# SSM input projections of a decoder step as three products of rounded parts

## The reference

```
cq, ckv, kr, z, xbc, dt, mq, g = split(x @ w_in)      # one input projection
o_mla = latent attention (8 heads) on cq, ckv, kr     # branch A
xbc   = silu(causal_conv(xbc)); y = ssd(xbc, dt) * silu(z); o_ssm = rms(y) # branch B, 4 groups of 8 heads
o_mem = attention of mq into 256 memory tokens        # branch M
m  = sig(gA)*(o_mla@WoA) + sig(gB)*(o_ssm@WoB) + sig(gM)*(o_mem@WoM)
x1 = LN(alpha*x + m@w_out);  y = LN(alpha*x1 + relu(x1@w_up+b)^2 @ w_down + b)
```

## Time and profile before

| | us |
|---|---|
| Median of 3 runs | 1787.76 (1786.57 to 1789.56) |
| The profiled execution's own time | 1788.35 |
| Its span in the trace | 1786.7 |
| PE busy in the span | 1712.9 (96%) |
| DVE / ACT / POOL busy | 734.7 / 379.3 / 370.1 |
| SSM stage, from the first matmul to the end of block 46 | 5.6 to about 495.5 |

### The profile page before, as it was taken

One profiled execution on the slowest core, in us unless ns is written; L12 is line 12 of the kernel. 1 busy time (PEld: TensorE's weight loads), 2 busy tenths in 40 slices (PEclk: granted clock), 3 DMA queues, 4 the chain that ended last, 5 costly groups with the idle time before them and its releaser, 6 DMA issues.

```text
span 1786.7 us, 25145 instructions
## 1 busy us (share of the span) xinstructions
PE 1712.9 (96%) x10132; PEld 1416.8 (79%) x10132; DVE 734.7 (41%) x1284; ACT 379.3 (21%) x758; POOL 370.1 (21%) x330
## 2 busy tenths in 40 slices
PE   8999999999999999999899999999996999999995
PEld 6767667677777877787677777778895999999995
DVE  5565667665341121111222212311157871157345
ACT  2151332514312121111011111100124111111122
POOL 0040221402210000000233210000034433434332
PEclk9999999999999999999999999999999999999998
DMA  5324224252253222221777775432221222222221
GB/s 211 116 77 142 89 78 148 77 174 66 85 192 110 65 61 70 71 71 42 236 232 247 239 256 186 156 106 71 72 95 36 83 89 89 84 94 83 89 78 50
DMA packets 70405, 206.18 MB, mean 115 GB/s; under 512 B 10161, under 2 KB 26802, under 8 KB 65682
## 3 DMA queue, kind: packets, MB, share of 16 engines
q1 hardware_dynamic: 50384, 151.67, 26.3%
q10 hardware_dynamic: 13762, 31.93, 5.2%
q0 software_dynamic: 6144, 20.98, 4.0%
HBM read 189.68 MB, written 14.86 MB: 114 GB/s over the span
## 4 chain that ended last, share of the span: by engine, by line
PE 90%; DVE 5%; DMA 2%; ACT 1%; issue 1%; SPq 1%; POOL 0%; POOLq 0%; ACTq 0%; DVEq 0%
PE acc L1638 37%; PE acc L1678 23%; PE acc L1939 6%; PE acc L1905 3%; PE bank L1849 2%; PE acc L1887 2%; PE acc L2042 1%; PE bank L1954 1%; PE bank L1973 1%; PE bank L1955 1%; PE bank L1809 1%; PE bank L2056 1%; PE bank L1924 1%; PE bank L1930 1%; PE bank L2127 1%
## 5 line engine op out<-in xcount | busy, mean ns | idle before, releaser
L1638 PE MATMUL acc<-xt,ring 128*128 128x272 f32 x2496 | 602.4, 399 | 3.2 <-DMA ring<-in_stream 3.2
L1638 PEld LDWEIGHTS acc<-xt,ring 128*128 128x128 f32 x2496 | 472.9, 192 | 124.6 <-issue 30.0
L485 POOL TENSOR_TENSOR f_parts<-ring,f_parts 128x1024 fp32r<-128x1024 f32 x72 | 173.4, 2409 | 392.7 <-ACT f_parts L662 392.7
L1678 PE MATMUL acc<-x_parts,f_parts 128*128 128x272 f32 x1664 | 236.7, 292 | 16.8 <-DVE x_parts L1085 11.2
L1678 PEld LDWEIGHTS acc<-x_parts,f_parts 128*128 128x128 f32 x1664 | 221.2, 191 | 19.9 <-issue 13.3
L1678 PE MATMUL acc<-f_parts 128*128 128x272 f32 x1536 | 194.3, 289 | 0.0
L1678 PEld LDWEIGHTS acc<-f_parts 128*128 128x128 f32 x1536 | 193.6, 188 | 0.2
L463 POOL DMA_DIRECT2D work<-in_page_cols x128 | 68.8, 538 | 475.1 <-PE bank L1994 365.5
L662 ACT ACTIVATE f_parts<-ring 128x1024 fp32r<-128x1024 f32 x72 | 76.5, 1062 | 336.2 <-PE acc L1678 331.9
L1939 PE MATMUL acc<-branch,ring 128*128 128x272 f32 x512 | 120.0, 392 | 0.0
L1939 PEld LDWEIGHTS acc<-branch,ring 128*128 128x128 f32 x512 | 96.0, 190 | 18.8
(11 more groups left out here) (329 smaller groups left out, 1822.1 us busy)
## 6 DMA issues: line engine op xcount, KB each, us to landing
ring<-in_stream SPq DMA_DIRECT2D x216, 512.0 KB, 3.6
work<-in_page_cols POOLq DMA_DIRECT2D x128, 160.0 KB, 3.4
attended<-in_ssm_state ACTq DMA_DIRECT2D x8, 1024.0 KB, 6.2
work<-cum_rows SPq DMA_DIRECT2D x32, 256.0 KB, 4.5
out_ssm_s<-attended ACTq DMA_DIRECT2D x8, 1024.0 KB, 5.6
work<-in_ckv_rows ACTq DMA_DIRECT2D x64, 128.0 KB, 3.6
work<-in_ckv_rows SPq DMA_DIRECT2D x64, 128.0 KB, 3.0
work<-in_memk_cols SPq DMA_DIRECT2D x8, 1024.0 KB, 6.5
```

What stands on the lines that cost most here:

```text
L485: pool.tensor_tensor(split[j][1], ring[:, s * BLOCK:(s + 1) * BLOCK], split[j][0].bitcast(F), SUB).then_inc(sem["split_ready"], 1)
L1638: m = pe.matmul(acc[p][:, half, 0:width], w[:, k * P:(k + 1) * P], x(kk)[:, half * width:(half + 1) * width], start=kk == 0, stop=kk == n_ ...
L1678: m = pe.matmul(acc_half, w[:, k * P:(k + 1) * P], x[:, kk, of], start=kk == 0 and n == 0, stop=kk == last and n == 2)
```

## The change

The 46 projections of the SSM stage (`project_x` in place of `project`) become three fp32r products as well, 48 matmuls a block in place of 16. Four things come with it.

1. Weights. After each evacuation of an accumulator ACT rounds a block into one of two buffers (`high_part`), and POOL subtracts it from the ring's slot in place (`low_part`). `high_part(n)` stands behind the evacuation of block n-2 and waits until PE has begun block n-1; PE begins block n when `low_part(n)` is done. POOL does 46 such subtractions between its other work.
2. x. Before block 1, ACT rounds the 8 chunks of x (128x544), DVE subtracts (8 operations, ahead of the dt work), and ACT rounds x once more over x itself, chunk by chunk, as PE's dt matmuls have taken each chunk. x is loaded again (2.2 MB, one DMA of SP) after the stage, as is the memory (1 MB, before at 38 us from ACT's queue, now from SP's when the last group's outputs are read out).
3. Buffers. `th` lies on `ext`, `rstd` on `sq_sum`, `b_mask` on `b_tm`. So `evac` of the third conv slice and on waits for the `finish` of the slice two before (`conv_ready`), and POOL's `b_mask` waits for the four state sums.
4. Waits that are merged or renamed (`vec_loaded` into `const_loaded`, `gate_a_ready` into `act_over`); DVE's first operation needs the constants in both kernels.

```
+            def high_part():
+                at = hi_at.next()
...
+                act.wait_ge(sem["blocks_begun"], CREDIT["blocks_begun"] + at)
+                act.wait_ge(sem[f"weights_in_slot{s}"], 16 * (loaded_before(at, s) + 1))
+                act.activation(w_hi[at % 2], ring[:, s * BLOCK:(s + 1) * BLOCK], ACT.Copy).then_inc(sem["hi_ready"], 1)
...
+            def low_part(n=1):
+                for _ in range(n):
...
+                    pool.wait_ge(sem["hi_ready"], t.next("hi_ready"))
+                    pool.tensor_tensor(ring_lo[:, slot], ring[:, slot], w_hi[at % 2].bitcast(F),
+                            SUB).then_inc(sem["split_ready"], 1)
...
             def evac(j):
+                n = evacuated.next()
+                if n > 2:
+                    act.wait_ge(sem["conv_ready"], n - 2)
                 act.wait_ge(sem[f"acc{j}_ready"], t.next(f"acc{j}_ready"))
...
+            for c in range(KC):
+                dve.wait_ge(sem["rounded"], t.next("rounded"))
+                dve.tensor_tensor(XL[:, c, :], X[:, c, :], XL[:, c, :].bitcast(F), SUB).then_inc(sem["normed_even"], 1)
...
+            def project_x(p, between=None):
...
+                pe.wait_ge(sem[f"acc{p}_free"], t.next(f"acc{p}_free"))
+                pe.wait_ge(sem["split_ready"], t.next("split_ready"))
+                for half, of in enumerate(halves):
...
+                    for k in range(KC):
+                        if at == 1 and half == 0:
+                            pe.wait_ge(sem["x_split"], t.next("x_split"))
+                        first, m = products(acc[p][:, half, 0:HT], wh, wl, XH, XL, k, k, KC - 1, of)
...
+            sp.wait_ge(sem["y_ready"], GC * GROUPS)
+            sp.dma_start(mem, mem_t).then_inc(sem["mem_loaded"], 16)
+            load(3)
+            sp.wait_ge(sem["blocks_begun"], CREDIT["blocks_begun"] + SSM_SPLIT + 2)
+            sp.dma_start(X, x_t).then_inc(sem["x0_loaded"], 16)
```

More of the change, by code:

```diff
@@ L136 @@
 SPLIT_FROM = blocks_before("out")
+SSM_SPLIT = blocks_before("mem_k") - 1
 def loaded_before(block, slot):
@@ L180, in sb, with raw @@
             return ctx.enter_context(nc.sbuf_tensor(name, [rows, cols], dt))
-        ring = sb("ring", RING * BLOCK)
+        with ExitStack() as as_loaded:
+            def raw(name, cols):
+                return as_loaded.enter_context(nc.sbuf_tensor(name, [P, cols], F))
+            ring, _, _, xt = raw("ring", RING * BLOCK), raw("at_cst", CW), raw("at_vecs", VW), raw("xt", KC * T)
+        ring_lo = sb("ring_lo", RING * BLOCK, R)
         cst = sb("cst", CW)
         vecs = sb("vecs", VW)
-        xt = sb("xt", KC * T)
+        xt_hi = sb("xt_hi", KC * T, R)
         mark = sb("mark", 2, F, 1)
@@ L248, in accv @@
             return acc[p][0:rows, :, 0:HT]
+        XH, XL = chunks(xt_hi, KC), chunks(ssm_parts, KC)
+        w_hi = [ssm_parts[:, KC * T + j * BLOCK:KC * T + (j + 1) * BLOCK] for j in range(2)]
         k = Carver()
-        ext, cacc, th = ([k(EXT) for _ in range(2)] for _ in range(3))
-        krope, a_rstd = k(T), k(T)
+        ext, cacc = ([k(EXT) for _ in range(2)] for _ in range(2))
+        th = [work[:, j * EXT + 3:(j + 1) * EXT + 3] for j in range(2)]
+        st_conv = k(NC * DEC_BATCH * 3).rearrange("p (c b t) -> p c b t", b=DEC_BATCH, t=3)
+        b_s = k(P, NS)
+        dec_p = k(NB * SSM_HEADS).rearrange("p (c h) -> p c h", h=SSM_HEADS)
+        k.at = 6 * T
+        off_s = k(GW)
+        c_mask = k(DEC_BATCH * NS).rearrange("p (b t) -> p b t", t=NS)
+        ecum_s = k(SSM_HEADS)
+        k.at = 6 * EXT
+        krope = k(T)
+        a_rstd = k(T)
         late_sq = [k(T) for _ in range(2)]
@@ L422, in _ @@
                         NS]), C("bmask").rearrange("p (b t) -> p b t", t=NS), MUL).then_inc(sem["c_masked"], 1)
+                low_part(2)
                 pool.wait_ge(sem["b_tm_read"], t.next("b_tm_read"))
+                pool.wait_ge(sem["add_ready"], t.next("add_ready", NB))
                 if g:
@@ L562, in _ @@
                 load()
-            load(blocks_before("sample") - blocks_before("mem_k"))
+            sp.wait_ge(sem["y_ready"], GC * GROUPS)
[3 more added lines that the diff above has]
+            sp.dma_start(X, x_t).then_inc(sem["x0_loaded"], 16)
+            load(blocks_before("sample") - blocks_before("mem_k") - 3)
             def cached_rows(b):
```

155 lines of the change are left out of this document (104 added, 51 removed).

## The result

| | before | changed |
|---|---|---|
| median of the runs | 1787.28 us (1786.57 to 1789.56, 4 runs) | 1810.48 us (1802.14 to 1812.08, 4 runs; a fifth, not in the median, took 1815.89) |
| ratio | | 1.0126, interval 1.0092 to 1.0161 |
| span of the profiled execution | 1786.7 us | 1800.5 us |

The forecast was 1780 us with a range of 1755 to 1798. The median lies 12 us above the range, and on the other side of no change. Both are used.

The account below looks back on a forecast made before the run. The prediction took PE to bound the kernel. Its terms, +9.3 -4.6 -5.8 -10.5 +2.5 +1.0 = -8.1 us against the profiled 1788.35, gave 1780 us with the median's 0.6 lower; range 1755 to 1798.

Parts of the forecast that it names:

- A group: Walk through one group of the SSM stage: second and third -2.9 us each, first -4.6, last -10.5.
- Clock and the end: PE's clock lowered by waits at group starts, +2.5 us; x's reload after the stage, +1.0; `b_mask`'s wait, nothing.
- the conv before the state additions: DVE's conv between block 12's evacuation and PE's first `state_adds`: longer beside POOL's operations and a subtraction, +1.0 us.
- the term put at nothing: POOL's `b_mask` waiting for the state sums, 25 us before `state_adds` wants it: no cost.
- What the products save: Each of 46 projection blocks takes 6.07 us instead of 7.41, saving 1.35 each, at most 62 us.
- DVE is not stopped: Rival for the SSM stage: POOL's subtractions do not delay DVE; groups about -6.5 us, total 1758 us; chance 22%.
- Before the first group: Stretch up to the first group: it starts at 77.4 us rather than 68.1, +9.3; without the lock 67.7.
- The first group: First group of the SSM stage: -4.6 us, since the slow clock lasted longer there before.
- The last group: Group without convs ahead: nine blocks -12.1 us, late `read_out` +1.6, together -10.5.
- The clock: PE's waits at group starts lower its clock for the time after: +2.5 us.
- The end, the reload of x: After the SSM stage: x's reload barely hidden behind three blocks, +1.0 us taken (0 to 4).
- The slower rival: POOL's queued operations and the subtraction precede DVE's next conv step: +7 us in three groups, 1801 us; chance 22%.

Follow-up runs that it names:

- three fills: Changed kernel with each POOL subtraction replaced by three fills with zeros that read nothing, the weights' remainder left out: 1772.13 us.
- small_low: Changed kernel with POOL subtracting only 16 of a block's 1024 columns, waits kept, third product using the rounded weights: 1760.40 us.
- the second profile: Profile of the changed kernel run again unaltered: median 1810.98 us, span 1808.0 us.
- small_high: Changed kernel with ACT rounding only 16 of a block's 1024 columns, POOL's subtraction whole: 1818.80 us.

## Why the prediction was wrong

**The steps that failed** are two terms of the section "A group" and of "Clock and the end". The first is the sentence on the conv before the state additions: "The conv now has half of the sample states' eight operations and a subtraction beside it; some of that was there before (four took 4.51 us), so +1.0." Evacuation to `state_adds` took 12.4 us, not 8.3: +5.1 in place of +1.0. The subtraction on 16 columns has 8.2 us there (+0.8) and the three fills 9.3 (+1.9), so about 3 of the 5.1 come from the subtraction's reads. The forecast stands on the assumption "each waiting for the other's whole instruction, and POOL getting in between two of DVE's". The first half is right. The second is too kind: POOL got in between DVE's steps every time (a subtraction, four L484 and an L476 beside the first conv), the subtractions also held DVE's operations ahead of the second conv and behind it, and elsewhere three POOL instructions in a row went ahead of one of DVE's.

The second is the term put at nothing: "`b_mask` waits for the state sums (POOL's 1.9 us), 25 us before `state_adds` wants it: nothing." Its result was not late, but its place was new. There it stands with a subtraction and a `scale_c` in POOL's queue and holds the masked product for 5.32 us, and PE waits 3.0 us at the first `read_out` in every group. Their neighbourhood was to be read in the order of instructions.

Counted from the start of the second group, the first state addition came at 62.0 us before, at 60.8 with the small subtraction and at 65.4 in the changed kernel; the forecast had it at 60.7. That is 4.7 of the 6.2 us by which this group missed its forecast. In the profiled executions the four groups together came out 26.6 us above their forecasts, of which the +2.5 taken for the clock covers a part, and the start and the end 2.2 us below.

Point by point:

- *What the products save.* A block takes about 6.1 us where PE's clock is full (72 records in 9.1 us), as forecast. With the small subtraction the whole takes 1760.4 us, where the rival "DVE is not stopped" said 1758. That is near by luck: it had the groups at -6.5 and the first group's start at -0.4; they came at -5.4, -3.8 and -3.8, and at -3.6.
- *Before the first group*: +9.3 forecast, +8.4 measured. But it came out by two errors: with fills of 2.23 us, which keep POOL's length and read nothing, it starts at 68.75 (forecast without the lock: 67.7), so the stop cost 7.7 us, not 9.7, and the rest came 1 us later than said. With the small subtraction it starts at 64.55, so POOL's length costs another 4.2 here.
- *The groups*: the subtraction costs 10.3, 7.1 and 7.0 us (changed minus small_low), where the forecast has 1.9 in the first and 3.6 in the others over its unstopped rival. Together with the last group (3.2 for 1.0) and the start, it costs 40 us in the profiled executions and 50 between the medians; 22 was forecast. Against the three fills, where its length is kept and only its reads are gone, it is 31 and 38 us: about that much is the stop.
- *The first group*: -4.6 forecast, +4.9 measured, the largest miss. The forecast took it to be slowed by the clock no more than the others; its clock is 0.90, and 0.94 in the next two.
- *The last group*: -10.5 forecast, -5.7 measured, -9.0 with the small subtraction. PE waits 3.0 us in it at the `read_out` behind the masked product and 1.7 for POOL.
- *The clock*: +2.5 forecast. The profiled execution's clock over the groups is 0.90 to 0.94 where it was 0.97 and 0.98; the second profile, at a lower clock, has PE busy for 2.6 to 4.6 us a group more in the first three. The term was of the right sign and too small; the runs don't separate it from the waits.
- *The end, the reload of x*: +1.0 forecast, 0 measured; the rest of the kernel is 1291.3, 1291.0 and 1290.2 us.
- *The slower rival* named the mechanism ("POOL's four back-to-back operations and the subtraction all go ahead of DVE's next step", +7 each, 1801, 22%). It had the place and nearly the size: by it the second and third group grow by 4.1 us, and they grew by 3.3 and 3.2 (4.8 and 6.4 in the second profile). It was given 22% because in rows 4 DVE got in between L447 and L451, a single case. It fell short of 1810 by the first group (+2.4 by it), the last group and the clock.
- *What was to be seen*: the first group's start (75 to 79: 76.5) and the conv steps (above 1.3: 1.35) came as said; group lengths (105 to 108 said, 112.8 to 115.8 found; 87 said for the last, 91.7 found) and the wait before `state_adds` (4 said, 7.0 found) did not. PE waited for POOL at two blocks a group, not one.

The Trainium skill, in SBUF — State Buffer, "SBUF: two separate sides", says that the shared pair of ports is "an exclusive lock, not a bandwidth split", taken by whichever starts first, for a DVE operation with two SBUF inputs only against a GpSimd one that reads SBUF. The runs agree in each part that they touch: the fill stops little (1080 ns for a step of 968), the subtraction a lot (1350), and a DVE operation with an operand in PSUM not at all (682 for 686). "Starts first" is not "is issued first": DVE's operation was issued at 215.98 and still came after the subtraction that began at 217.53. The prediction used the rule, and what it got wrong is how often DVE has to wait, not that it does.

## What to carry to other kernels

Before work is moved to POOL, look at what DVE does beside it. Here a POOL operation with two operands from SBUF cost DVE up to its whole length and, with more of POOL's work queued behind, several lengths, while a fill, or a DVE operation with an operand in PSUM, lost next to nothing. Price such a change by DVE's longest chain that PE waits for, not by PE's saving, and read POOL's queue for neighbours without a wait between them, those too that a new layout of buffers has moved. To test the suspicion cheaply, shrink the suspected instruction to 16 columns with all its handovers kept, and add it alone to the old kernel.

## What the runs showed that was not expected

- DVE can be passed over: 5.32 us for an operation of 0.69 behind three POOL instructions in a row, 5.47 behind four; at other places the two take turns one by one.
- Less work on ACT made the kernel 8 us slower (small_high); POOL's subtractions then met other DVE operations.
- Splitting a POOL instruction into four, at 43% more POOL time (4 x 0.95 against 2.65 us), made the kernel 13 us faster.
- A TENSOR_SCALAR with a single tensor from SBUF is stopped too: 128x24 in 1.93 us at 233.71, and the conv's first step in 1472 ns on the mean (664 before) with the subtractions in the kernel before.
- A POOL fill of 128x1024 takes 0.96 us, the subtraction of the same size 2.4 to 2.7.
